# TensorE's expert loop: one width choice per item, three passes looped inside each width's code, six widths from 128 columns, loop head aligned to 16 KB

## The chip, the core and the metric

The kernel runs on one core of a Trainium2 chip. The metric is the device time of one launch in microseconds, the median of three runs. Beside it stands one profiled execution, from which all rows below are read.

## What is computed

One decoder block on 1024 tokens of width 1024 in fp32: a combined projection, four heads of differential attention and four of a chunked mLSTM, an output projection, then a mixture of experts and a final norm. The change touches the mixture of experts alone. Each token picks its top 4 of 32 experts; each expert is a clamped SwiGLU of width 1024:

```python
def expert_block(args):
    rows, e = args
    xb = xt[rows]
    gu = xb @ w_gu[e] + b_gu[e]                      # 1024 -> 2048
    glu = jnp.minimum(gu[:, :D_FF], SWIGLU_LIMIT)
    lin = jnp.clip(gu[:, D_FF:], -SWIGLU_LIMIT, SWIGLU_LIMIT)
    act = glu * jax.nn.sigmoid(SWIGLU_ALPHA * glu) * (lin + 1)
    return act @ w_down[e] + b_down[e]               # 1024 -> 1024
```

The results are weighted by the gates and added to the token rows. The numbers of tokens per expert depend on the data, 4096 in all.

## The kernel before

Everything is one hand-written program for each engine, joined by semaphores; there is no scheduler, so each engine executes what the source says in that order. Some 640 us go into projections, attention, mLSTM and routing. Then comes the loop over items. An item is one expert with up to CAP = 224 of its tokens; experts with more would get further items, up to 18, which are handled by a second loop in which the width is always 224.

TensorE keeps the weights stationary, in blocks of 128x128, and streams the item's token columns. An item is three passes: two halves of gate and up (each gives 512 gate and 512 up features), then the down projection. A pass is 64 matmuls in four slabs of 1 MB of weights, one for each of four slots; every matmul of fp32 operands is executed as two, each with its own weight load, so a pass leaves 128 matmul records in the trace. SyncE (L410) refills a slot as soon as the pass's last matmul on it signals `slab_done`. ScalarE (L1265, L1276, L1259) and VectorE (L1821, L1836, L1839) take the results out of PSUM, add biases and form the activation; VectorE transposes rows in and out (L1774, L1793) and scales the next item's columns (L1782); GpSimd gathers token rows (L560) and adds results to DRAM (L581). These engines always work on the full 224 or 256 columns. Only TensorE looks at the item's true number of tokens, `n_now`: the table `WIDTHS` lists the widths for which the four-slab code exists, and `by_width` walks down a tree of branches (lines 962 to 970) to the narrowest code that holds n.

In `one_pass` (L989 on) a register `phase` tells the pass within the item. L992 and L1001 branch on it: in phase 0 the item's registers are set, in phase 1 the next item's token count is loaded from SBUF (L1002), in phase 2 the registers are moved to the activation's columns. Then `by_width` chooses the code, whose matmul is L1024 with the width w fixed in it, and L1034 advances the count `moved`, against which slots and banks are waited for. The whole is one loop of 96 rounds (L1046), so that head, phase branches and width tree are passed in each of the three passes.

The waits in the four-slab code are those for the columns (`rhs_ready`), the slot (`slot_in`, L1017 and L1021) and the bank (`bank_read`).

## Time and profile before

| | us |
|---|---|
| median of 3 runs | 2265.82 |
| lowest, highest | 2259.61, 2268.32 |
| the profiled execution | 2265.43 |
| its span, first to last instruction | 2263.6 |
| TensorE matmul busy (PE) | 2192.9 |
| VectorE busy (DVE) | 1413.0 |
| ScalarE busy (ACT) | 565.9 |
| matmuls of line L1024, first and last start | 652.5, 2239.0 |

PE is TensorE's matmul side, PEld its weight loads, which run beside matmuls, PEldq and PEq its sequencer's own instructions (branches, register operations). Busy times of PE are those of overlapping records: a record of L1024 lasts 276 ns and more, while the next one starts after 112 to 190 ns. For the pace one therefore takes the time of a stretch over the count of its records. "issue" as the reason of idle time means that the engine waited for nothing that the profile shows.

### The profile page before, as it was taken

The numbers are of one execution on the slowest core, as the hardware profiler recorded it, in microseconds if no ns is written. First come the engines' busy times: TensorE is split into PE (matmuls) and PEld (weight loads), VectorE is DVE, ScalarE is ACT, GpSimd is POOL, SyncE is SP. The second block draws the span as 40 slices with busy tenths as digits, with TensorE's granted clock in tenths as the row PEclk, the third lists the DMA queues.
The fourth block names the chain that finished last, engine by engine and source line by source line (L and its number), as shares of the span: only waits on it lengthen the run. The fifth ranks groups of instructions, "written<-read, shape, count | busy, mean of one in ns | idle before, by whom it ended". The sixth has DMA issues, their size and how long they took to land.

```text
span 2263.6 us, 40201 instructions
## 1 busy us (share of the span) xinstructions
PE 2192.9 (97%) x14677; PEld 1893.8 (84%) x14679; DVE 1413.0 (62%) x2880; ACT 565.9 (25%) x1240; POOL 258.3 (11%) x235
## 2 busy tenths in 40 slices
PE   8999999999978999999999999999999999999996
PEld 4444554566668999999999999999999999999996
DVE  3352231678684777777778677764755566667567
ACT  2122221344311222222222222321221122222123
POOL 1000000121230110111001000110100000001013
PEclk9999999999988999999999999999999999999998
DMA  8000011210165899989989888976976788788688
GB/s 312 34 38 0 0 38 40 98 58 29 67 210 175 282 306 306 304 283 307 312 277 311 282 282 305 311 256 210 304 262 224 235 278 286 244 294 295 232 257 294
DMA packets 244662, 488.92 MB, mean 216 GB/s; under 512 B 24572, under 2 KB 24780, under 8 KB 244452
## 3 DMA queue, kind: packets, MB, share of 16 engines
q1 hardware_dynamic: 223684, 452.48, 57.3%
q0 software_dynamic: 20704, 35.60, 7.1%
q8 instruction: 34, 0.56, 0.1%
q10 hardware_dynamic: 224, 0.16, 0.0%
q14 instruction: 16, 0.13, 0.0%
HBM read 477.67 MB, written 49.63 MB: 233 GB/s over the span
## 4 chain that ended last, share of the span: by engine, by line
PE 92%; DVE 4%; issue 1%; ACT 1%; DMA 1%; POOL 0%; DVEq 0%; SPq 0%; POOLq 0%; ACTq 0%
PE PS L1024 66%; PE PS L664 15%; PE PS L851 5%; PE PS L791 1%; PE PS L824 1%; DVE pairA L1793 1%; PE PS L813 1%; PE PS L870 0%; DMA pairB<-acc_dram 0%; DVE unit L1522 0%; DVE pairA L1839 0%; PE PS L736 0%; DVE unit L1833 0%; PE PS L659 0%; PE PS L637 0%
## 5 line engine op out<-in xcount | busy, mean ns | idle before, releaser
L1024 PE MATMUL PS<-pairA,unit 128*128 x12288 | 1563.1, 290 | 31.3 <-DVE pairA L1839 11.9
L1024 PEld LDWEIGHTS PS<-pairA,unit 128*128 128x128 f32 x12288 | 1554.5, 191 | 40.0 <-issue 39.4
L1774 DVE STREAM_TRANSPOSE unit<-unit 32x512 f32<-32x512 f32 (+1 forms) x512 | 325.5, 636 | 10.3 <-DMA unit<-h_dram,cur_x 3.0
L1793 DVE STREAM_TRANSPOSE pairA<-unit 32x512 f32<-32x512 f32 (+1 forms) x512 | 325.8, 636 | 7.1
L664 PE MATMUL PS<-pairA,unit 128*128 128x512 f32 (+1 forms) x528 | 231.1, 594 | 1.4 <-issue 1.4
L1276 ACT ACTIVATE unit<-PS,cur_b 128x256 f32<-128x256 f32 x256 | 107.5, 471 | 414.9 <-PE PS L1024 414.9
L560 POOL DMA_INDIRECT unit<-h_dram,cur_x x66 | 68.8, 1042 | 1184.4 <-DVE cur_x L1829 1160.5
L664 PEld LDWEIGHTS PS<-pairA,unit 128*128 128x128 f32 (+1 forms) x528 | 97.4, 188 | 116.1 <-issue 115.4
L1259 ACT ACTIVATE unit<-unit 128x512 f32<-128x512 f32 x128 | 80.6, 630 | 453.8 <-DVE unit L1821 453.8
L1265 ACT ACTIVATE unit<-PS,cur_b 128x256 f32<-128x256 f32 x256 | 107.4, 471 | 317.7 <-PE PS L1024 314.2
L1813 DVE COPY cur_b<-b_all 128x24 f32 x32 | 6.7, 209 | 265.2 <-ACT unit L1276 261.3
L1836 DVE TENSOR_SCALAR unit<-unit 128x512 f32<-128x512 f32 x128 | 54.5, 426 | 167.0 <-ACT unit L1265 164.1
L1821 DVE TENSOR_SCALAR unit<-PS,cur_b 128x256 f32<-128x256 f32 x256 | 108.7, 478 | 40.7 <-PE PS L1024 38.6
L581 POOL DMA_INDIRECT acc_dram<-pairA,cur_y x64 | 102.8, 1606 | 211.4 <-ACT pairA L1251 201.0
L664 PE MATMUL PS<-unit,pairA 128*128 128x512 f32 x256 | 112.0, 595 | 0.3 <-ACT unit L1115 0.3
L664 PEld LDWEIGHTS PS<-unit,pairA 128*128 128x128 f32 x256 | 48.0, 190 | 59.5 <-issue 58.2
L1833 DVE TENSOR_TENSOR unit<-unit 128x512 f32<-128x512 f32 x128 | 88.4, 691 | 8.8
L1839 DVE SCALAR_TENSOR_TENSOR pairA<-unit 128x512 f32<-128x512 f32 x128 | 88.7, 693 | 4.4
L1251 ACT ACTIVATE pairA<-pairA,g_now 128x512 f32<-128x512 f32 x128 | 81.6, 715 | 1.8 <-DVE pairA L1793 1.8
L1782 DVE TENSOR_TENSOR pairA<-unit,vec 128x448 f32<-128x448 f32 x128 | 71.4, 620 | 0.0
L1522 DVE CUSTOM_DVE_ANT_0 unit<-PS,unit 128x128 f32<-128x128 f32 (+7 forms) x64 | 48.0, 750 | 29.2 <-PE PS L791 29.2
L1192 ACT ACTIVATE unit<-unit,small 128x128 f32<-128x128 f32 (+7 forms) x64 | 49.4, 772 | 51.5 <-DVE small L1525 51.0
(252 smaller groups left out, 1130.6 us busy)
## 6 DMA issues: line engine op xcount, KB each, us to landing
unit<-in_expert_w_gu_dram SPq DMA_DIRECT2D x256, 1024.0 KB, 5.1
unit<-in_expert_w_down_dram SPq DMA_DIRECT2D x128, 1024.0 KB, 8.2
unit<-in_w_in_dram SPq DMA_DIRECT2D x6, 2048.0 KB, 15.9
pairB<-in_x_dram SPq DMA_DIRECT2D x16, 512.0 KB, 5.9
unit<-in_w_out_dram SPq DMA_DIRECT2D x2, 2048.0 KB, 8.9
h_dram<-pairA SPq DMA_DIRECT2D x8, 512.0 KB, 2.6
acc_dram<-pairB SPq DMA_DIRECT2D x8, 512.0 KB
pairB<-acc_dram SPq DMA_DIRECT2D x8, 512.0 KB, 7.9
```

What stands on the lines that cost most here:

```text
L581: pool.indirect_dma_start(out=acc_dram, out_offset=bass.IndirectOffsetOnAxis(ap=cur_y[:, b:b + 1], axis=0), in_=y_rows[:, b, :], in_offset ...
L664: ins = pe.matmul(ps, lhs, rhs, start=(k == 0), stop=(k == KD - 1))
L851: ins = pe.matmul(ps, (da_mixT, ml_mixT)[k // 4][:, k % 4, P * t:P * t + P], w_o[k // 4][:, k % 4, HALF * half:HALF * half + HALF], start= ...
L1024: ins = pe.matmul(ps[:, ITEM * (j % 2):ITEM * (j % 2) + w], slot_w[s][:, k, P * j:P * j + P], xa_cols[:, ITEM * kd:ITEM * kd + KD * ITEM + ...
L1251: act.activation(half, half, ACT.Identity, scale=g_now[:, q // 2, :]).then_inc(y_evac, 1)
L1265: ins = act.activation(lin_b[:, b, ITEM * j:ITEM * j + ITEM], bank(2 + b)[:, ITEM * j:ITEM * j + ITEM], ACT.Identity, bias=cur_b[:, f:f + 1])
L1276: ins = act.activation(yT[:, 2 * s + j, :], bank(s)[:, ITEM * j:ITEM * j + ITEM], ACT.Identity, bias=cur_b[:, 2 * NF + 2 * s + j:2 * NF + ...
L1774: ins = dve.transpose(cols[:, :, :, 32 * q:32 * q + 32], rows[:, :, :, 32 * a:32 * a + 32])
L1793: ins = dve.transpose(rows[:, :, :, 32 * a:32 * a + 32], cols[:, :, :, 32 * q:32 * q + 32])
L1821: ins = dve.tensor_scalar(glu_t[:, b, ITEM * j:ITEM * j + ITEM], bank(b)[:, ITEM * j:ITEM * j + ITEM], cur_b[:, f:f + 1], LIMIT, ALU.add, ...
L1833: step.do(dve.tensor_tensor(glu_s[:, b, :], glu_t[:, b, :], glu_s[:, b, :], ALU.mult))
L1839: dve.scalar_tensor_tensor(out=actT[:, 2 * c:2 * c + 2, :].rearrange("p j n -> p (j n)"), in0=lin_c[:, b, :], scalar=1.0, in1=glu_s[:, b, ...
```

## The change

Only TensorE's program changes. The table of widths gets six entries, 128, 140, 152, 168, 184 and 224, instead of five, 132, 148, 168, 184 and 224. The register `phase` goes. The outer loop has one round per item, 32 in all: at its head the item's registers are set, the width is chosen once, and inside the code of each width stands a loop of three passes, at whose start one branch sees whether this is the third (then the registers move on to the activation's columns). The next item's token count is loaded in every pass. The columns' half is read from its register in each pass. Before the outer loop stands an alignment: the loader fills up so that the loop's first instruction lies at a multiple of 256 instructions (16 KB). Since the tree still splits off the first width first, the order of the codes in memory is 224, 184, 168, 152, 140, 128.

```diff
--- before.py
+++ after.py
@@ -53,7 +53,7 @@
 LISTS = 2 * (ROUNDS + 1)
 CAP_BITS = 21
 CAP_MUL = (1 << CAP_BITS) // CAP + 1
-WIDTHS = [132, 148, 168, 184, CAP]
+WIDTHS = [128, 140, 152, 168, 184, CAP]
 SLOTS = 4
 NO_ROW = 1 << 20
 
@@ -974,64 +974,63 @@
             turn_early((1, 2, 3))
             place(NT - 1)
             add_rows(NT - 2)
-            n_now, n_next, phase, moved, first_half, all_eight, half, item = (pe.alloc_register(n) for n in (
-                "n_now", "n_next", "phase", "moved", "first_half", "all_eight", "half", "pe_item"))
+            n_now, n_next, moved, first_half, all_eight, half, item = (pe.alloc_register(n) for n in (
+                "n_now", "n_next", "moved", "first_half", "all_eight", "half", "pe_item"))
             pe.wait_ge(items_ready, 1)
             pe.load(n_next, item_n[0:1, 0:1])
             pe.reg_mov(n_now, SEQ)
-            for reg, value in ((moved, 16), (first_half, 4), (all_eight, 0), (half, 0), (phase, 0), (item, 0)):
+            for reg, value in ((moved, 16), (first_half, 4), (all_eight, 0), (half, 0), (item, 0)):
                 pe.reg_mov(reg, value)
             add_rows(NT - 1)
             pe.wait_ge(h2T_ready, 2 * NT)
             pe.wait_ge(place_read, NT)
             pe.wait_ge(b_ready, 2)
 
-            def one_pass(widths):
-
-                p = pe.snap(phase, min_val=0, max_val=2)
-                with pe.If(p < 1):
-                    pe.reg_mov(n_now, n_next)
-                    pe.reg_add(item, item, 1)
-                    pe.reg_add(first_half, all_eight, 2)
-                    pe.reg_add(all_eight, all_eight, 4)
-                    pe.reg_mov(half, 0)
-                    pe.reg_mov(phase, 1)
-                with pe.Else():
-                    nxt = pe.snap(item, min_val=1, max_val=ITEMS)
-                    with pe.If(p < 2):
+            def four_slabs(w):
+
+                block0 = pe.snap(half, min_val=0, max_val=KD * ITEM)
+                for s in range(SLOTS):
+                    side, low = s // 2, s % 2 == 0
+                    if side == 0:
+                        pe.wait_ge(rhs_ready, first_half if low else all_eight)
+                    pe.wait_ge(slot_in[s], moved)
+                    for j in range(4):
+                        ps = bank(2 * side + j // 2)
+                        if low and j % 2 == 0:
+                            pe.wait_ge(bank_read[2 * side + j // 2], moved)
+                        for k in range(4):
+                            kd = k if low else 4 + k
+                            ins = pe.matmul(ps[:, ITEM * (j % 2):ITEM * (j % 2) + w],
+                                            slot_w[s][:, k, P * j:P * j + P],
+                                            xa_cols[:, ITEM * kd:ITEM * kd + KD * ITEM + w][:, bass.ds(block0, w)],
+                                            start=(low and j % 2 == 0 and k == 0), stop=(not low and k == 3),
+                                            skip_group_check=True)
+                        if not low and j == 1:
+                            ins.then_inc(low_bank_done[side], 1)
+                    ins.then_inc(slab_done[s], 1)
+
+            def one_item(widths):
+
+                pe.reg_mov(n_now, n_next)
+                pe.reg_add(item, item, 1)
+                pe.reg_add(first_half, all_eight, 2)
+                pe.reg_add(all_eight, all_eight, 4)
+                pe.reg_mov(half, 0)
+                n = pe.snap(n_now, min_val=0, max_val=SEQ)
+                nxt = pe.snap(item, min_val=1, max_val=ITEMS)
+
+                def three_passes(w):
+
+                    with pe.Fori(0, 3) as p:
+                        with pe.If(p > 1):
+                            pe.reg_add(first_half, all_eight, 2)
+                            pe.reg_add(all_eight, all_eight, 4)
+                            pe.reg_mov(half, KD * ITEM)
                         pe.load(n_next, item_n[0:1, bass.ds(nxt, 1)])
-                        pe.reg_mov(phase, 2)
-                    with pe.Else():
-                        pe.reg_add(first_half, all_eight, 2)
-                        pe.reg_add(all_eight, all_eight, 4)
-                        pe.reg_mov(half, KD * ITEM)
-                        pe.reg_mov(phase, 0)
-                n = pe.snap(n_now, min_val=0, max_val=SEQ)
-                block0 = pe.snap(half, min_val=0, max_val=KD * ITEM)
-
-                def four_slabs(w):
-                    for s in range(SLOTS):
-                        side, low = s // 2, s % 2 == 0
-                        if side == 0:
-                            pe.wait_ge(rhs_ready, first_half if low else all_eight)
-                        pe.wait_ge(slot_in[s], moved)
-                        for j in range(4):
-                            ps = bank(2 * side + j // 2)
-                            if low and j % 2 == 0:
-                                pe.wait_ge(bank_read[2 * side + j // 2], moved)
-                            for k in range(4):
-                                kd = k if low else 4 + k
-                                ins = pe.matmul(ps[:, ITEM * (j % 2):ITEM * (j % 2) + w],
-                                                slot_w[s][:, k, P * j:P * j + P],
-                                                xa_cols[:, ITEM * kd:ITEM * kd + KD * ITEM + w][:, bass.ds(block0, w)],
-                                                start=(low and j % 2 == 0 and k == 0), stop=(not low and k == 3),
-                                                skip_group_check=True)
-                            if not low and j == 1:
-                                ins.then_inc(low_bank_done[side], 1)
-                        ins.then_inc(slab_done[s], 1)
-
-                by_width(n, widths, four_slabs)
-                pe.reg_add(moved, moved, 16)
+                        four_slabs(w)
+                        pe.reg_add(moved, moved, 16)
+
+                by_width(n, widths, three_passes)
 
             def turn_last():
                 for side in range(2):
@@ -1043,8 +1042,9 @@
                                                yT[:, 4 * side + m, P * (q // 2):P * (q // 2) + P], ident[:, :])
                         ins.then_inc(y_ps, 1)
 
-            with pe.Fori(0, 3 * N_EXP):
-                one_pass(WIDTHS)
+            pe.addr_align(256)
+            with pe.Fori(0, N_EXP):
+                one_item(WIDTHS)
             pe.wait_ge(items_ready, 2)
             last = pe.value_load(n_items[0:1, 0:1], min_val=N_EXP, max_val=ITEMS)
             with pe.If(last <= N_EXP):
@@ -1052,8 +1052,7 @@
             with pe.Else():
                 with pe.Fori(N_EXP, ITEMS) as extra:
                     with pe.If(extra < last):
-                        with pe.Fori(0, 3):
-                            one_pass([CAP])
+                        one_item([CAP])
                 turn_last()
```

How the built program's instructions stand on TensorE, at the entry of the loop (the last matmuls of L957 come before it), before:

```order
L957 MATMUL PS<-unit,pairA 128x224 x8
L1046 UNCONDITIONAL_BRANCH
L992 COMPARE_AND_BRANCH
L993 ISA
L992 UNCONDITIONAL_BRANCH
L1001 COMPARE_AND_BRANCH
L1002 ISA
L1002 TENSOR_LOAD item_n
L1001 UNCONDITIONAL_BRANCH
L1005 ISA
L1004 UNCONDITIONAL_BRANCH
L1009 ISA
```

and now:

```order
L957 MATMUL PS<-unit,pairA 128x224 x8
L1045 ISA
L1046 UNCONDITIONAL_BRANCH
L1014 ISA
L1019 ISA
L967 COMPARE_AND_BRANCH x4
L1024 UNCONDITIONAL_BRANCH
L1025 COMPARE_AND_BRANCH
L1026 ISA
L1025 UNCONDITIONAL_BRANCH
L1029 ISA
L1029 TENSOR_LOAD item_n
```

The phase branches are gone, the width branches L967 stand at the head of the item, and the load of `item_n` has moved behind them, into the code of each width (here that of 224).

The end of the loop on TensorE, from the last matmuls of the narrowest width on, before:

```order
L1024 MATMUL PS<-pairA,unit 128x132 x45
L969 UNCONDITIONAL_BRANCH
L1034 ISA
L1046 COMPARE_AND_BRANCH
L1049 TENSOR_LOAD n_items
```

and now:

```order
L1003 MATMUL PS<-pairA,unit 128x128 x45
L1031 ISA
L1024 COMPARE_AND_BRANCH
L969 UNCONDITIONAL_BRANCH
L1046 REGISTER_ALU
L1046 COMPARE_AND_BRANCH
L1049 TENSOR_LOAD n_items
```

The count `moved` is advanced within the width's code, followed by the branch back to the next pass (L1024 of the new source); only then comes the branch back to the head (L1046).

## Rows read from the trace of the kernel before

**Rows 1.** The page: busy time, chain by line, costliest groups (busy us, mean ns | idle).

```profile
PE 2192.9 (97%) x14677; PEld 1893.8 (84%) x14679; DVE 1413.0 (62%) x2880; ACT 565.9 (25%) x1240; POOL 258.3 (11%) x235
...
PE PS L1024 66%; PE PS L664 15%; PE PS L851 5%; PE PS L791 1%; PE PS L824 1%; DVE pairA L1793 1%; PE PS L813 1%; PE PS L870 0%; DMA pairB<-acc_dram 0%; DVE unit L1522 0%; DVE pairA L1839 0%; PE PS L736 0%; DVE unit L1833 0%; PE PS L659 0%; PE PS L637 0%
...
L1024 PE MATMUL PS<-pairA,unit 128*128 x12288 | 1563.1, 290 | 31.3 <-DVE pairA L1839 11.9
```

**Rows 2.** Waits 740 to 2240 us: us in total, times, longest us.

```profile
PE PS L1024 <- DVE pairA L1839: 3.1, 8, 0.6
...
PE PS L1024 <- issue: 3.1, 17, 0.2
...
SPq L410 <- PE PS L1024: 1275.7, 364, 5.5
```

**Rows 3.** Windows, one item each: 132, 148, 168, 224 columns wide.

```profile
core 0: us, PE busy (x) PEld busy (x) DVE busy (x) ACT busy (x) POOL busy (x), PEclk, DMA share, GB/s
774.16:817.88 43.72, 43.53 (x386) 43.34 (x385) 33.29 (x61) 11.68 (x24) 5.28 (x4) 1.00 0.93 304
1129.90:1179.60 49.70, 48.96 (x386) 48.52 (x386) 33.57 (x61) 11.68 (x24) 5.29 (x4) 1.00 0.84 276
1266.90:1322.10 55.20, 55.07 (x387) 54.82 (x386) 33.56 (x61) 11.68 (x24) 5.29 (x4) 1.00 0.77 251
1496.90:1569.60 72.70, 72.70 (x387) 72.70 (x386) 33.55 (x61) 11.68 (x24) 5.28 (x4) 1.00 0.58 194
```

**Rows 4.** Timeline of PE at the loop's start: start, us, group [idle before <-releaser].

```profile
652.47 18.12 PE L1024 MATMUL PS<-pairA,unit 128*128 x128 [7.59 <-issue]
679.41 18.29 PE L1024 MATMUL PS<-pairA,unit 128*128 x128 [8.82 <-DVE pairA L1839]
705.31 18.98 PE L1024 MATMUL PS<-pairA,unit 128*128 x128 [7.60 <-DVE pairA L1782]
724.45 16.37 PE L1024 MATMUL PS<-pairA,unit 128*128 x128 [0.16 <-issue]
```

**Rows 5.** Branches L967 in 642:650, 670:680, 697:703 us: ns min/median/max.

```profile
L967 PEldq COMPARE_BRANCH  x3: 73/4437/4711, 642.9 to 647.8; - x3
...
L967 PEldq COMPARE_BRANCH  x3: 68/232/7974, 670.7 to 678.9; - x3
...
L967 PEldq COMPARE_BRANCH  x3: 73/2987/4719, 697.1 to 702.0; - x3
```

**Rows 6.** The same branches from 730 to 2240 us.

```profile
L967 PEldq COMPARE_BRANCH  x186: 65/202/210, 740.5 to 2224.1; - x186
```

**Rows 7.** DMA queues, 640 to 730 us: the instruction queue of TensorE is q8.

```profile
q8 instruction: 13, 0.21, 1.1%
```

**Rows 8.** The same queue in 0:640 and 2240:2263 us, and on the page, whole span.

```profile
q8 instruction: 19, 0.31, 0.2%
...
q8 instruction: 2, 0.03, 0.6%
...
q8 instruction: 34, 0.56, 0.1%
```

**Rows 9.** Windows of the first three passes.

```profile
652.40:679.40 27.00, 18.12 (x128) 17.90 (x128) 22.26 (x41) 6.45 (x11) 6.73 (x6) 0.82 0.60 202
679.40:705.30 25.90, 18.29 (x128) 18.08 (x128) 16.87 (x30) 2.94 (x6) 2.75 (x2) 0.83 0.47 164
705.30:724.40 19.10, 18.98 (x128) 18.77 (x128) 1.60 (x4) 2.59 (x7) 0.00 (x0) 0.86 0.45 159
```

**Rows 10.** Timelines: weight loads of L870, matmuls of L824.

```profile
456.31 1.86 PEld L870 LDWEIGHTS PS<-rw,pairA 128*128 128x128 f32 x16 [0.76 <-DVE pairA L1582]
...
458.60 1.06 PE L824 MATMUL PS<-unit 128*128 128x128 f32 x8
```

**Rows 11.** L1034 at the end of the first pass.

```profile
L1034 PEldq FUSED_REGOPS  x1: 42/42/42, 668.5 to 668.5; - x1
```

**Rows 12.** Windows: the last item.

```profile
2195.40:2239.10 43.70, 43.51 (x386) 43.32 (x385) 37.22 (x68) 13.04 (x26) 8.54 (x8) 1.00 0.96 331
```

## The prediction

> **What bounds the kernel now.** I read the page first. TensorE is busy for 2192.9 us, 97% of the span, and 66% of the chain that ended last is one line, the matmul of the expert loop, L1024 [rows 1]. The waits, taken from 740 us on, say the same from the other side: TensorE waits 3.1 + 3.1 us at it, and SyncE's weight transfers wait for it to free a slot 1275.7 us in total [rows 2]. So from the second item on, a nanosecond taken from each matmul record, or from the instructions between two passes, comes off the time one for one, while VectorE, ScalarE, GpSimd and the DMA only follow.
>
> Next the price of a column. A matmul of this fp32 kernel has two records, each with its own weight load, so an item (three passes of 64 matmuls) has 384. One item each of four of the five widths stands in [rows 3]. The 224-wide item takes 72.70 us with TensorE busy throughout: 189.3 ns a record. Two cycles of 2.4 GHz for each of 224 columns are 186.7 ns, which leaves 2.6 ns. By that, 384 records cost 43.24 us at 132 columns, 48.36 at 148, and 54.76 at 168; the rows have 43.72, 49.70 and 55.20. What is over, 0.48, 1.34 and 0.44 us, is what the branches and register work between passes cost an item. It is largest at 148 columns, whose code lies behind three branches.
>
> Then the start of the loop, which looks quite different. Before the first pass TensorE stands still for 7.59 us, before the second for 8.82, before the third for 7.60 [rows 4]. The name of VectorE on two of them is no reason to blame it: the width branches L967, normally 0.07 to 0.21 us each [rows 6], took up to 4.7, 8.0 and 4.7 us in just these places [rows 5]. They wait for code: 13 instruction fetches fall between 640 and 730 us, and none in the 1510 us after that: 19 before 640 and 2 after 2240 us make up the page's 34 [rows 7, 8]. The three passes take 27.00 + 25.90 + 19.10 = 72.0 us where 48.4 would do; part of this is a granted clock of 0.82 to 0.86, the mean of stretches at 2.4 and at 1.2 GHz after each standstill [rows 9].
>
> **The change, part by part.** Which item gets which width needs the number of tokens of each expert. They follow from the reference's router on its inputs: 139, 138, 60, 61, 114, 114, 145, 77, 129, 120, 134, 122, 117, 149, 116, 80, 80, 128, 217, 110, 143, 174, 181, 168, 118, 161, 168, 117, 108, 184, 156, 68. No expert is over 224, so there are 32 items, as [rows 1] has it (12288 = 32 x 384). The widths move like this:
> - 139, 138 and 134 go from 148 to 140: 8 columns x 0.833 ns x 384 = 2.56 us each, -7.7 us.
> - 145 and 143 go from 148 to 152: +1.28 us each, +2.6 us.
> - 149 goes from 168 to 152: -5.1 us.
> - 129 goes from 132 to 140, as 128 no longer holds it: +2.6 us.
> - The other 17 items of the old 132 go to 128. By columns alone each would gain 4 x 0.833 x 384 = 1.28 us, 21.8 us in all. I don't believe it. In the router's matmul L870 only 32 columns move, yet its 16 weight loads follow each other at (1.86 - 0.19) / 15 = 111 ns, and L824, which is exactly 128 columns on 128x128 fp32 weights, runs at (1.06 - 0.275) / 7 = 112 ns [rows 10]. So a weight load sets a floor of about 111.5 ns, against 112.6 ns at 132 columns. The gain is 1.1 ns x 384 x 17 = 7.2 us.
> - 168, 184 and 224 stay.
>
> The sum is -14.8 us; with no floor it would be -29.4 us. The Trainium skill has a rule on the other side: TensorE: Matmul & The Clock Gate (the Trainium skill, section "Wait — 56ns, not 53.3ns?") gives N / 2.4 GHz plus about 2.5 ns between matmuls of N columns. The constant agrees with the 2.6 ns of [rows 3]; carried down to 128 columns it says 109.3 ns and the -29.4 us, which L870 and L824 speak against.
>
> *Between the passes.* The phase tests L992 and L1001 and two of three walks down the width tree disappear; a pass now ends in a branch back to its own code. An item passes the head once. There it does what the second pass did before, branches and the load of `item_n` included, and the load now also runs in every pass. The sequencer works ahead of the matmuls (L1034 is done at 668.5 us, the matmuls of that pass end at 652.47 + 18.12 = 670.6) [rows 4, 11], so about 2 us of such work are hidden, and the pass-internal way, with one branch back, one test and one load, is shorter than that. I price an item at 0.45 us over its records, as 132 and 168 have now. That changes nothing for those; for the five items that leave 148 it is 1.34 - 0.45 = 0.9 us each: -4.5 us. The bounds are 0 (the one remaining walk costs as much as three) and -6 us. The cover is the run ahead; if it were gone, 32 heads at some 2 us would cost 60 us, but nothing in the change takes it away.
>
> *Code.* In the built programs the loop has 1375 instruction slots before and 1713 now, without padding. A block of code is 16 KB, 256 slots: 19 fetches go with the some 5000 instructions ahead of the loop [rows 8]. So there are 5.4 blocks before, 6.7 now. From an aligned head these are seven, and at many other phases they would touch eight. The head is in block 0, the body of 140 columns in blocks 4 and 5, that of 128 in 5 and 6; each body lies in two blocks, and its three passes stay there. The first gap should remain: the first item (139) again meets two branches into code not yet there, 4.7 + 4.4 us before, the same now. The second and third gaps came at returns to the head between passes of one item; these returns are gone. They, with the half clock behind them, are 72.0 - 48.4 - (18.12 - 16.37, the slow part of the first pass) = 21.9 us [rows 9]. But the code that the branches waited for there was mostly code fetched once already, shortly before: 13 fetches for a loop of six or seven blocks. The store seems to take blocks in order and to throw away what was put in the wrong place until a whole round has run in order. The new loop has more far jumps in another order: over blocks 1 to 3 in the first items, and into 1 to 3 when 217, 174 and 168 come, which fetches block 2 late. I put this at four more waits of one fetched block each, 4.4 to 4.7 us: 18.5 us. The net is -3 us. The bounds are -21.9 us (nothing fetched twice) and +15 us (eight such waits).
>
> **Sum**, against the profiled execution of 2265.4 us (span 2263.6 us; the median of the runs, 2265.8 us, is practically the same): 2265.4 - 14.8 - 4.5 - 3 = 2243.1 us. What is next behind TensorE doesn't come in: a narrow item moves 304 GB/s with the DMA engines at 0.93 [rows 3], and at 43.3 instead of 43.7 us it would be 307, where another stretch has 331 GB/s [rows 12].
>
> **The rivals.**
> - *The code doesn't stay in store (slower).* Seven blocks, and the one fetched ahead behind the last, make eight. The trace shows only that six or seven stay [rows 8]. If eight don't, the successor of the last block throws out the head's, and every item waits for at least one block: 31 x 4.6 = 143 us, at the worst 31 x 8.0. Time: 2265.4 - 14.8 - 4.5 - 21.9 + 143 = 2367 us or more. For it: the tight fit, and blocks fetched twice even with fewer. Against it: nothing was fetched in 1510 us though all five widths were used. It decides from the first block that has no place. Chance 0.12. The Trainium skill says two different things here. Advanced Engine Details and Errata (the Trainium skill, section "ISA Cache") gives 128 KB on TensorE in lines of 16 KB, thus eight, and the alignment would just do. Runtime: NRT & Kernel Launch (the Trainium skill, section "Instruction fetch mechanics") speaks of a window of two pages, outside which a taken branch stalls for a fetch; that would be this rival, and [rows 8] speak against it.
> - *Nothing is fetched twice.* With the returns inside an item gone, the store fills in order. 2265.4 - 14.8 - 4.5 - 21.9 = 2224 us. For it: later jumps mostly land in blocks just used. Against it: the two repeats before. Chance 0.2.
> - *Settling costs more than it did:* eight or more waits, or slabs that come late after them. 2265.4 - 14.8 - 4.5 + 15 = 2261 us, up to 2285. Chance 0.14.
> - *No floor from the weight loads.* The 17 items gain all 21.8 us: 2243 - 14.6 = 2228.5 us. Against it two lines of the trace. Chance 0.06.
>
> **How the numbers follow.** The forecast, 2243 us, within 2232 to 2262, has 0.48. A measurement of this kernel tells 0.5% (11 us) from no change, so faster is below 2254.5 and slower above 2277. Faster: most of the forecast (0.40), the second and the fourth rival (0.26): 0.66. Same: the forecast's upper edge (0.08) and most of the third rival (0.11): 0.19. Slower: the rest of the third (0.03) and the first (0.12): 0.15. The range goes from 2222 us, the case without repeats, to 2277 us, and leaves out the first rival and the edges.
>
> **What would show it.** In the changed kernel's trace, the start distance of matmul records in a 128-column item: 111.5 ns and an item of 43.3 us (right), 109.3 ns and 42.4 us (no floor). Items of 140 columns at 46.3 us, of 152 at 50.1. One gap of 7 to 11 us before the first pass, none before the second and third. The width branches at their usual 0.07 to 0.21 us but for some four of 3 to 8 us at heads of items, with as many code fetches outside the first 90 us. If instruction fetches go on all through the loop, the first rival holds and the forecast is wrong; if there are none after the first item, the second.

## The result and the profile after

The changed kernel takes **2291.7 us** (median of six executions, 2287.6 to 2305.0) against 2265.9 us of the kernel before beside it: a ratio of 1.0128 (95% interval 1.0111 to 1.0145; ratios and intervals below are meant the same way, each against the kernel before in the same batch). It is slower by 1.3%; the prediction had 2243 us, 2222 to 2277. The profiled execution has a span of 2285.6 us, 22.0 us more than before's 2263.6.

The page after: busy time, the queue of TensorE's instruction fetches (q8), and the matmul of the expert loop, now line L1003 (busy us, mean ns | idle time before them and what ended most of it).

```profile
PE 2187.0 (96%) x14677; PEld 1889.3 (83%) x14679; DVE 1413.9 (62%) x2880; ACT 565.3 (25%) x1240; POOL 258.4 (11%) x235
...
q8 instruction: 43, 0.70, 0.1%
...
L1003 PE MATMUL PS<-pairA,unit 128*128 x12288 | 1556.2, 290 | 61.2 <-issue 59.2
```

Against [rows 1] the matmuls are busy 6.9 us less, so the narrower widths did arrive, but the idle time before them has doubled, from 31.3 to 61.2 us, and nearly all of it ends in "issue": TensorE waits for no other engine, its own sequencer has nothing for it. 43 blocks of code are fetched instead of 34 [rows 8]; a packet of q8 is one block of 16 KB.

Windows of one item each after, 128, 140, 152 and 224 columns wide (columns as in [rows 3]):

```profile
767.90:811.30 43.40, 43.12 (x385) 42.93 (x385) 33.38 (x61) 11.35 (x24) 5.28 (x4) 1.00 0.92 304
1126.90:1173.30 46.40, 46.02 (x384) 45.81 (x384) 33.52 (x61) 11.36 (x24) 5.28 (x4) 1.00 0.87 294
1260.40:1310.40 50.00, 49.83 (x384) 49.60 (x384) 33.48 (x61) 11.28 (x24) 5.28 (x4) 1.00 0.83 273
1484.30:1557.10 72.80, 72.77 (x385) 72.77 (x386) 33.55 (x61) 11.21 (x24) 5.27 (x4) 1.00 0.58 189
```

These are the lengths that were forecast: 43.3, 46.3 and 50.1 us, and 224 columns as before. An undisturbed item is as short as it should be; the loss is elsewhere. The timeline of TensorE at the loop's start (start, us, group, idle before) shows the first place:

```profile
656.62 48.96 PE L1003 MATMUL PS<-pairA,unit 128*128 x384 [12.11 <-issue]
718.56 48.71 PE L1003 MATMUL PS<-pairA,unit 128*128 x384 [12.98 <-issue]
767.85 12.32 PE L1003 MATMUL PS<-pairA,unit 128*128 x108 [0.58 <-issue]
```

The first item's three passes run through, where before stood gaps of 8.82 and 7.60 us between them [rows 4]. But a gap of 12.98 us has come between the first item and the second. The second place lies where before had nothing at all [rows 6, 8]. From 1480 us on, the branches L967 (ns min/median/max), TensorE's waits (us, times, longest) and the instruction queue:

```profile
L967 PEldq COMPARE_BRANCH  x38: 65/68/6062, 1482.6 to 2210.7; - x38
...
PE PS L1003 <- issue: 28.0, 10, 6.3
...
q8 instruction: 12, 0.20, 0.1%
```

In before's trace the same stretch of the loop (1480 to 2239 us) has not one fetch and 0.9 us of such waits:

```profile
PE PS L1024 <- issue: 0.9, 5, 0.2
```

The fetches begin 18 us into the item of 217 rows, the first that is 224 columns wide, and six of the branches that follow take 3.4 to 6.1 us. Five of the six cost more than they take, since TensorE's clock is down behind them; behind the one of 3.81 us at 1836.9 the granted clock stays at 1.00. Windows behind the branch of 4.35 us at 1599.2 and behind the one of 3.42 us at 1655.6 (the granted clock is the figure behind the five busy times):

```profile
1605.00:1608.00 3.00, 2.98 (x12) 2.98 (x13) 2.10 (x3) 0.00 (x0) 0.00 (x0) 0.50 0.06 23
...
1660.30:1678.00 17.70, 17.66 (x95) 17.66 (x96) 8.16 (x17) 1.26 (x2) 2.08 (x2) 0.83 0.37 129
```

0.50 is 1.2 GHz, 0.83 a mixture of both levels.

To say what each part costs I take, for every item, the time from its first matmul record to the next item's, and subtract 384 records at their undisturbed length (2 x width / 2.4 GHz + 2.5 ns, and 111.5 ns at least). What is left over is standstill (for code, and now and then for a slab of weights), slow clock and the work between passes. "Columns" is the sum of what was subtracted, a calculated figure and not a measured one. Items count from 0; "late" stands below for items 18 to 31, which begin at about 1480 us. In us, with the fetches of code from the first matmul of the loop on in brackets, for all kernels of this case but e12 (each from its one profiled execution, which for e3, e5 and e7 is the slowest of its runs):

```
                 widths picked  aligned | start  columns  items 0-1  items 2-17  items 18-31 | last matmul
before              5   pass       no   | 652.5   1545.0  25.1 (11)    9.8 (0)     6.8 (0)   | 2239.0
after               6   item      yes   | 656.6   1530.8  19.7 (7)    12.0 (1)    42.8 (12)  | 2261.7
e1_five             5   item      yes   | 657.8   1545.0  17.3 (7)     9.6 (1)     6.0 (0)   | 2235.6
e2_noalign          6   item       no   | 655.0   1530.8   3.9 (2)    11.4 (0)    20.4 (5)   | 2221.3
e3_chain            6   item      yes   | 664.8   1530.8   5.0 (3)    25.8 (0)    18.0 (0)   | 2244.3
e4_linger           6   item      yes   | 657.2   1530.8  17.8 (7)    13.0 (1)    46.0 (12)  | 2264.6
e5_skip             6   item      yes   | 656.5   1530.8   4.3 (2)    12.9 (0)    56.2 (14)  | 2260.5
e6_chain208         6   item  at 208    | 660.0   1530.8  50.4 (19)  383.2 (138) 112.4 (45)  | 2736.6
e7_off229           6   item  at 229    | 657.4   1530.8   4.9 (2)    11.5 (0)    58.4 (19)  | 2262.9
e8_five130_free     5   item       no   | 654.0   1534.8   5.7 (3)    12.7 (0)     7.3 (0)   | 2214.4
e9_five_free        5   item       no   | 654.4   1545.0   5.2 (3)    10.2 (0)     7.6 (0)   | 2222.3
e10_six_alone       6   pass       no   | 654.3   1530.8  35.0 (11)   12.7 (0)    60.1 (18)  | 2292.8
e11_align_alone     5   pass      yes   | 658.3   1545.0   5.9 (3)     9.8 (0)     7.1 (0)   | 2225.8
e13_walk            6   item      yes   | 668.9   1530.8   3.8 (2)    12.9 (0)     9.3 (0)   | 2225.5
e14_walk130         6   item      yes   | 667.3   1525.9   5.6 (2)    12.0 (0)     7.5 (0)   | 2218.3
```

The first two rows are the account of the change: start +4.1, columns -14.2, items 0 and 1 -5.4, items 2 to 17 +2.2, items 18 to 31 +36.0, which makes +22.7 us at the last matmul; 0.7 us come back behind it. The change of the columns can be checked against measured time in items 2 to 17, where nearly nothing is fetched: together they take 722.7 us before and 716.5 after, 6.3 us less, and the account has -8.5 for their columns and +2.2 for the rest.

### The profile page after: what moved, and what is told of

The parts are those of the page before. It is cut to its first block, busy times and chain, and to the rows that moved or that the text cites. A ratio compares the mean times of both kernels' runs of the same rounds, so it can differ in the third digit from the quotient of the medians.

```text
span 2285.6 us, 40116 instructions
## 1 busy us (share of the span) xinstructions
PE 2187.0 (96%) x14677; PEld 1889.3 (83%) x14679; DVE 1413.9 (62%) x2880; ACT 565.3 (25%) x1240; POOL 258.4 (11%) x235
## 4 chain that ended last, share of the span: by engine, by line
PE 93%; issue 3%; DVE 1%; DMA 1%; ACT 1%; SPq 0%; POOL 0%; POOLq 0%; DVEq 0%; ACTq 0%
PE PS L1003 67%; PE PS L664 15%; PE PS L851 5%; PE PS L791 1%; PE PS L824 1%; DMA pairB<-acc_dram 1%; PE PS L813 1%; PE PS L870 0%; DVE unit L1521 0%; PE PS L736 0%; PE PS L659 0%; PE PS L637 0%; DMA pairB<-in_x_dram 0%; PE PS L957 0%; PE PS L724 0%
## 5 line engine op out<-in xcount | busy, mean ns | idle before, releaser
L1003 PE MATMUL PS<-pairA,unit 128*128 x12288 | 1556.2, 290 | 61.2 <-issue 59.2
L1003 PEld LDWEIGHTS PS<-pairA,unit 128*128 128x128 f32 x12288 | 1549.2, 193 | 68.5 <-issue 68.2
```

What stands on the lines that cost most here:

```text
L1003: ins = pe.matmul(ps[:, ITEM * (j % 2):ITEM * (j % 2) + w], slot_w[s][:, k, P * j:P * j + P], xa_cols[:, ITEM * kd:ITEM * kd + KD * ITEM + ...
```

## The experiments

Blocks are counted from the loop's head: block 0 holds the head, the aligned loop of six widths lies in 0 to 6, the body of 224 columns in 0 and 1, 184 in 1 and 2, 168 in 2 and 3, 152 in 3 and 4, 140 in 4 and 5, 128 in 5 and 6 (from the built program).

### First round: what of the change brings the stalls

After the comparison of the traces I had a theory (A in the expectations that follow): the store has eight places in a ring; whoever enters a block has the next one fetched into the place behind it; a branch to a block that isn't there has it put into the place behind the current one, whatever stands there. The trace shows when a block is fetched, but neither which one nor where it is put, so this is a model. With the order in which the changed kernel visits its blocks it gave 23 fetches in the loop, as many as the trace has from 640 us to the loop's end. The others say that the size decides, or the structure.

**e1_five.**

```diff
-WIDTHS = [128, 140, 152, 168, 184, CAP]
+WIDTHS = [132, 148, 168, 184, CAP]
```

> The changed kernel with the old five widths (132, 148, 168, 184, 224), so 5.6 blocks of loop code instead of 6.7. Theory A (order of the store: it holds eight blocks of 16 KB, a block that is fetched goes behind the one the sequencer runs in, and what stood there is lost, so far jumps in a new order throw out code that is needed): 11 code fetches in the loop, all before 780 us, none from 780 to 2240 us; the waits from the 19th item on, about 42 us, go, the wider code costs 13 us more: 2263 us. Theory B (capacity: seven blocks and the one fetched ahead don't fit, five widths do): the same 2263 us. Theory C (the new loop form, not its code size, is what costs): the late waits stay, 2290 us or more.

2264.5 us (ratio 1.0006, 0.9991 to 1.0021), as A and B both had it, so this run doesn't tell them apart; C is refuted. With one width less the late fetches are gone, 6.0 us over the columns in items 18 to 31 as in before, although the structure and the alignment are the changed kernel's. Its waits from 1480 to 2200 us:

```profile
PE PS L1003 <- issue: 3.0, 7, 0.7
```

The first item's stall stays.

**e2_noalign.**

```diff
-            pe.addr_align(256)
```

> The changed kernel without the alignment before the loop: the head then lies some 165 instructions into a block and the loop touches eight blocks instead of seven. Theory A: 18 fetches in the loop instead of 23 and fewer late branches that wait (items 20 to 24 instead of 20 to 32), no padding to run through before the loop: about 2270 us. Theory B: with eight blocks and one ahead even less fits, so fetches go on in nearly every item: over 2300 us. Theory C: 2285 us, the padding's few us less.

**2247.9 us** (ratio 0.9932, 0.9909 to 0.9956): without its alignment the changed kernel is faster than before, and 44 us faster than with it. None of the figures foresaw that, mine being 22 us too high. The loop touches eight blocks now instead of seven and stalls less, so a mere count of blocks, by which B had over 2300 us, is refuted. It isn't free of late stalls either: five late fetches come in items 18 to 23, with branches of 4.4 and 3.6 us ahead of items 20 and 21, the first two of the five items that theory A named. Of the 18 fetches that A gave the loop, however, only 11 came.

**e3_chain.**

```diff
-                near = 1 if widths[0] == WIDTHS[0] else len(widths) // 2
+                near = len(widths) - 1
```

> The changed kernel with the tree of width branches made a chain: n over 184, else over 168, else over 152 and so on, so that the branches walk through the blocks in the order in which they lie in memory. Same six widths, same seven blocks, aligned. Theory A: 7 fetches in the loop, none after the first item, so both the reload in the second item (16 us) and the late waits (42 us) go; up to five taken branches per item instead of one to three cost 0.2 us each, some 20 us over all items: 2254 us. Theory B: the same bytes don't fit, the fetches stay: 2290 us or more, with the longer chain rather 2310 us.

The widths are tried one after the other from the widest down; each test stands at the head of the body that it chooses, so whoever wants the narrow code passes all blocks. 2266.2 us (1.0014, 0.9999 to 1.0029). There is no late fetch, with the same seven blocks, but the tests cost a narrow item about 1.1 us more, and the loop starts 8 us later. The seven fetches are what A said, the time is 12 us above its figure. Two waits of over 2 us are left in items 24 and 27, and they are not for code: the sequencer stands 2.50 and 2.21 us at L1000, and what ends both waits is the landing of a slab of weights. The first of them, too, has 3.4 us at a granted clock of 0.50 behind it.

**e4_linger.**

```diff
             pe.addr_align(256)
+            for _ in range(6):
+                pe.load(n_next, item_n[0:1, 0:1])
```

> The changed kernel with six loads of a register (0.3 us each) between the alignment and the loop, so that TensorE's sequencer stays in the head's block for about 2 us before its first far branch and the next block is under way by then. Theory A: the first far block then goes behind it, nothing has to be loaded again in the second item: 18 fetches in the loop instead of 23, TensorE's gap between item 1 and 2 (13 us) falls under 1 us, the late waits stay; 2291.7 - 16 + 2 = 2278 us. Theory B: 23 fetches or more, 2293 us.

2291.8 us in two executions, as the changed kernel (1.0127), with the same fetches. But the edit didn't do what it was meant to. Of the six loads only one stands in the trace:

```profile
L1047 PEldq TENSOR_LOAD <-item_n x1: 487/487/487, 648.3 to 648.3; - x1
```

The first slow branch comes at 649.4 instead of 648.5 us, so the sequencer stayed 0.9 us longer in the head's block and not some 2 us. That 0.9 us change nothing is shown; whether 2 us would, as A says, was not tested.

### Second round: is it the place of the code?

**e5_skip.** The alignment fills the rest of the block ahead of the loop with instructions that do nothing, and the changed kernel runs through them. Its trace has 92, within 6.7 us:

```profile
L1045 PEldq NOP  x92: 13/13/13, 641.2 to 647.9; - x92
```

```diff
-            pe.addr_align(256)
+            pe.addr_align(256, max_nops=0)
```

> The changed kernel with its padding branched over instead of executed (the 92 padding instructions were executed between 641.15 and 647.88 us of the changed kernel's span, about 71 ns each). Theory A, the padding costs what it takes: the loop's first matmul comes at 650 us instead of 656.6 and the time falls by 6 to 7 us, to 2285. Theory B, the padding runs beside the fetch of the loop's first blocks, which would be waited for otherwise (without any alignment the loop starts at 655.0, only 1.6 us earlier): the loop starts at 654 to 656 and the time is 2289 to 2292. In both, the late stalls stand where they stood in the changed kernel, since no block lies elsewhere.

The branch over the padding is there (one, at 642.8 us) and the loop's counter is set at 643.2 instead of 647.9 us, but the first matmul comes at 656.5 us, as before the edit (656.6). So B on this point: the padding ran beside fetches that are waited for in any case. The time, however, is 2274.8 us, with ten executions from 2266.9 to 2286.3, which neither theory had. The profiled one is the slowest of them: its first items are clean (4.3 us) and its late ones worse than the changed kernel's (56.2 us, 14 fetches), though not one instruction lies elsewhere. So the addresses alone don't decide what is fetched late. That it is how the first fetches fell in time is the nearest explanation; no run tests it by itself.

**e6_chain208.** e3_chain, moved by 208 instructions:

```diff
-            pe.addr_align(256)
+            pe.addr_align(256, offset=208)
```

> Descending chain of widths as in e3_chain, but the loop's head at instruction 208 of its 16 KB block, so that the code touches eight blocks instead of seven. Theory R (eight places in a ring; entering a block fetches the block behind it into the next place; a branch to a block that isn't there puts it into the next place): the block behind the last one of the loop, fetched ahead for nothing, takes the place of the head block, so that nearly every item's end branches to a block that isn't there: about 36 missed branches and 129 fetches in the loop instead of 8, each miss 3.3 to 4.5 us and up to 3 us of half clock behind it: 2380 to 2460 us. Theory C (what counts is whether the loop's blocks fit into eight): eight fit, nothing is fetched again, 2264 to 2275 us.

**2763 us**, in one execution. The loop touches blocks 0 to 7 now. TensorE between 800 and 1010 us:

```profile
801.85 44.83 PE L1003 MATMUL PS<-pairA,unit 128*128 x384 [24.39 <-issue]
869.75 45.00 PE L1003 MATMUL PS<-pairA,unit 128*128 x384 [23.07 <-issue]
937.59 45.20 PE L1003 MATMUL PS<-pairA,unit 128*128 x384 [22.84 <-issue]
```

and the page, with the branches L967 from 730 us on:

```profile
q8 instruction: 227, 3.72, 0.6%
...
L1003 PE MATMUL PS<-pairA,unit 128*128 x12288 | 1597.6, 295 | 493.5 <-issue 491.2
...
L967 PEldq COMPARE_BRANCH  x140: 70/3096/5968, 775.4 to 2686.8; - x140
```

At the ends of the first 18 items TensorE stands for 17 to 29 us, but for one: seven to eleven blocks are fetched in each of these items (three in the last), one after the other, and the median branch takes 3.1 us. Same instructions, same order, 497 us more than e3_chain. Eight blocks don't stay when the items walk through them; seven do. That a ninth, fetched ahead for nothing, is what is too much fits the nine fetches that most of the first narrow items have, but isn't shown by itself. C is refuted. R is right in kind and far too mild: it had 129 fetches in the loop where 207 came, and 2460 us at most.

Advanced Engine Details and Errata (the Trainium skill, section "ISA Cache") gives TensorE 128 KB in lines of 16 KB, thus eight; the same section has "Only 2 cache lines!" beside it, which the seven blocks that stay in e3 contradict. Eight places agree with e3 and e6 if one of them goes to the block ahead. Runtime: NRT & Kernel Launch (the Trainium skill, section "Instruction fetch mechanics") has a taken branch stall whenever its target isn't in the current window of two pages; in e1_five the branches go from block 0 to block 4 for more than 1400 us and nothing is fetched, so this does not hold here.

**e7_off229.**

```diff
-            pe.addr_align(256)
+            pe.addr_align(256, offset=229)
```

> The changed kernel with its loop starting at instruction 229 of a 16 KB block instead of 0: same code, same order, eight blocks touched as without the alignment (instruction 165). Theory R: the fetches come out at 33 in the loop, with missed branches after items 19, 20, 22, 23, 24, 26, 27, 28 and 30 about (11 in all after the first item, against 6 in the changed kernel): 2305 to 2325 us. Theory U (an unaligned loop is good and an aligned one bad, whatever the cause): like the kernel without the alignment, 2246 to 2255 us. Theory C (eight blocks fit): the same as U.

2282.6 us (1.0077, 1.0045 to 1.0110), four executions from 2276.3 to 2289.4. The loop is as little aligned as in e2_noalign, which starts at instruction 165 of its block, and has 58.4 us late instead of 20.4 (in the slowest of the four, the profiled one). So it isn't alignment against none; each place of the code has its own stalls. R's figure was 22 us too high (24 fetches, not 33), U's 27 too low.

**e8_five130_free.**

```diff
-WIDTHS = [128, 140, 152, 168, 184, CAP]
+WIDTHS = [130, 146, 168, 184, CAP]
...
-            pe.addr_align(256)
```

> Five widths (130, 146, 168, 184, 224), passes looped inside each width, no alignment. 130 columns take 110.8 ns by columns, below the 111.5 ns that the 128-column records show, so 130 costs what 128 costs and takes item 8 (129 rows) in; the columns' sum of the loop is 1534.9 us against 1544.96 of before's widths and 1530.8 of the six. Theory R puts no missed branch behind the second item with this size and start: overhead as in e1_five behind its second item (15.7 us) and as in e2_noalign ahead (4 us), loop from 655 to 2209, span 2233 to 2237, time 2235 to 2239. Theory U/C: the same, as the code is smaller. If the second walk through the blocks that e1_five showed after its first item (12.4 us) comes here too: 2247 to 2251.

**2241.4 us** (0.9914, 0.9883 to 0.9946), the fastest of all, 19.6 us below the kernel before beside it. L967 and the waits from 1480 to 2200 us:

```profile
L967 PEldq COMPARE_BRANCH  x34: 65/169/210, 1544.0 to 2170.0; - x34
PE PS L1003 <- issue: 2.7, 6, 0.7
```

No branch over 0.21 us. It gives up 4.1 us of the six widths' columns and has nothing of their stalls. The forecast of R was 2 us too low.

### Third round: each part alone

**e9_five_free**, the loop over passes alone (e8 with before's widths):

```diff
-WIDTHS = [130, 146, 168, 184, CAP]
+WIDTHS = [132, 148, 168, 184, CAP]
```

> One part alone: the width picked once per item with the three passes looped inside, but before's five widths and no alignment. Column sum 1544.96 us, 10.1 more than e8_five130_free (2241.36), everything else the same code in the same places. Theory R (no missed branch behind the second item, seven blocks): 2250 to 2253 us, a gain of 10 to 13 us over before that comes from the first item's two stalls of 8 to 9 us and the half clock behind them. Rival (the loop over passes gives nothing, e8's gain is its widths): 2258 to 2263.

2252.6 us (0.9956, 0.9937 to 0.9974), 11 us above e8, whose columns are 10.1 less. The time is in R's range. The gain over before, 8.9 us between the medians, lies where it was said to, in the first items: 5.2 instead of 25.1 us. The later start (1.9 us) takes some of it back.

**e10_six_alone**, the widths alone, on the kernel before:

```diff
-WIDTHS = [132, 148, 168, 184, CAP]
+WIDTHS = [128, 140, 152, 168, 184, CAP]
```

> One part alone: six widths in before's structure (the width picked again in each pass, no alignment, eight blocks touched). Columns give 14.2 us. Theory R: eight blocks and a ninth fetched ahead don't fit into eight places, so that from item 18 on branches miss again, 5 to 10 times at 5 to 6 us each beside before's first item: 2275 to 2305 us. Theory W (six widths are what they are by columns, the stalls of the changed kernel come from its structure or its alignment): 2251 to 2256.

**2324.8 us** (1.0289, 1.0246 to 1.0332). Its page:

```profile
q8 instruction: 51, 0.84, 0.2%
...
L1024 PE MATMUL PS<-pairA,unit 128*128 x12288 | 1569.1, 291 | 77.7 <-issue 74.5
```

W is refuted: with neither the loop over passes nor the alignment the sixth width brings 60.1 us of late stalls, 20 us more than the range of R, and 35.0 us in the first items.

**e11_align_alone**, the alignment alone, on the kernel before:

```diff
+            pe.addr_align(256)
             with pe.Fori(0, 3 * N_EXP):
                 one_pass(WIDTHS)
```

> One part alone: before with its loop aligned to a 16 KB block, nothing else (six blocks touched). Theory R: behind the first item no block is fetched; the padding runs beside fetches and costs 1 to 4 us at the loop's start, the first item's stalls are 12 to 24 us as in before: 2258 to 2270 us. Theory U (the alignment is what costs, some 40 us as between the changed kernel and e2_noalign): 2290 to 2310.

**2251.7 us** (0.9943, 0.9923 to 0.9963), below both ranges. TensorE in the first item:

```profile
658.27 19.03 PE L1024 MATMUL PS<-pairA,unit 128*128 x128 [12.88 <-issue]
678.17 16.37 PE L1024 MATMUL PS<-pairA,unit 128*128 x128 [0.87 <-issue]
```

The gap ahead of the second pass is 0.87 us, where before has 8.82 [rows 4], with the very same returns to the head. The alignment, which costs the changed kernel 44 us, gives before 10 (difference of the medians) to 13 (by the ratio).

**e12_floor96** tests the floor of a record. On e2_noalign, the body of the narrowest width multiplies 96 columns instead of 128:

```diff
             def four_slabs(w):
+                u = 96 if w == 128 else w
...
-                            ins = pe.matmul(ps[:, ITEM * (j % 2):ITEM * (j % 2) + w],
+                            ins = pe.matmul(ps[:, ITEM * (j % 2):ITEM * (j % 2) + u],
```

(and the columns of the second operand likewise)

> e2_noalign whose narrowest code multiplies only 96 of its 128 columns (columns 96 to 127 of the 17 items that run in it are left out of the product, so those rows' outputs are not the reference's). Theory F (a matmul of this kernel is never shorter than loading its 128 by 128 float32 weights, 111.5 ns): a record stays at 111.5 to 111.7 ns, an item at 43.4 us, the time at 2248. Theory N (the records follow the columns down): 82.5 ns a record inside a slab, which would leave such an item to its transfers at about 38 us or less, and the time at 2060 to 2160.

2248.1 us in one execution; e2_noalign has 2247.9. A window of one such item:

```profile
1380.80:1424.20 43.40, 43.12 (x385) 42.96 (x385) 33.35 (x61) 11.70 (x25) 5.28 (x4) 1.00 0.92 309
```

43.40 us for 384 records, as the 128 columns take in e2_noalign and in the changed kernel; inside the slabs a record starts 111.7 ns after the other in all three, so it isn't the transfers that hold them. A quarter fewer columns gives nothing, and N is refuted. The floor goes with the load of 128 x 128 float32 weights, which is what these records share with those of L870, 111 ns apart with 32 columns moved [rows 10]. The rule of N / 2.4 GHz + 2.5 ns (the Trainium skill, TensorE: Matmul & The Clock Gate, section "Wait — 56ns, not 53.3ns?") would have 82.5 ns for such a record, at the two cycles a column that [rows 3] show; that section doesn't count the load, so it doesn't hold here.

### Fourth round: why seven blocks don't stay

e3_chain kept seven blocks, the changed kernel did not. Either the order in which the first items bring them in decides, or the chain's habit of passing all of them each time.

**e13_walk.**

```diff
-                near = 1 if widths[0] == WIDTHS[0] else len(widths) // 2
+                near = 1 if widths[0] == WIDTHS[0] else len(widths) - 1
```

> The changed kernel (six widths, aligned) with one change in the tree of branches: 128 columns are reached by one branch as there, the others by a descending chain, so that the first item (139 rows) passes the blocks 1 to 5 in order before its passes. Theory O (what decides is that the blocks come in once, in order; the late fetches come from block 2, which the changed kernel's first items jump over): no code fetch behind 720 us, items 18 to 31 within 10 to 18 us over their columns instead of 42.8, the loop starts at about 665 us as in e3_chain: 2244 to 2256 us. Theory D (e3_chain is free of late fetches only since every item walks the blocks and so keeps them; a jump from block 0 to blocks 5 and 6 throws something out): late fetches as in the changed kernel, 2285 to 2300.

**2253.0 us** (0.9947, 0.9928 to 0.9965), 39 us below the changed kernel. The same from 1480 to 2200 us:

```profile
L967 PEldq COMPARE_BRANCH  x46: 65/169/210, 1480.2 to 2181.2; - x46
PE PS L1003 <- issue: 5.8, 10, 1.4
```

Its page, whole span:

```profile
q8 instruction: 27, 0.44, 0.1%
```

O, then. The 17 items of 128 columns jump from block 0 to block 5 as in the changed kernel, which by D should have thrown something out. The items with wider code take another way, down the chain; the first item does so through blocks 1 to 5 in order, and from the second item's start (717.8 us) to the end of the loop nothing is fetched, so later walks can have brought nothing in. Nor is it luck in time as in e5_skip, as far as executions tell: the ten of e5_skip and the six of the changed kernel all lie above 2266 us, the four of this kernel between 2252.1 and 2255.4.

How the order does it is the model's account. In the changed kernel the first items jump from 0 to bodies in 4 to 6 by way of 3. Block 2 isn't needed until the item of 217 rows has its successor fetched (the fetch at 1502.6 us); by the model it comes into a full ring, out of order, and throws out a block in use, whose return throws out the next: twelve fetches and six waits up to the end. The price of the walk is the start, 12.3 us later.

**e14_walk130** is e13_walk with widths 130, 140, 150, 168, 184, 224:

```diff
-WIDTHS = [128, 140, 152, 168, 184, CAP]
+WIDTHS = [130, 140, 150, 168, 184, CAP]
```

> e13_walk with widths 130, 140, 150, 168, 184, 224. The columns' sum falls from 1530.8 to 1525.9 us (the 129-row item into the 130-column code, whose records cost the floor of 111.5 ns; three items from 152 to 150). Theory O: 4.9 us below e13_walk, 2239 to 2251, about even with e8_five130_free (2241.36). Theory D: 2280 to 2295.

2246.7 us (0.9917, 0.9899 to 0.9935): 6.3 us less than e13_walk, 4.9 by its columns. By its ratio it is level with e8_five130_free.

## Why the prediction was wrong

*Widths: right.* Forecast -14.8 us with a floor of 111.5 ns; the account has -14.2, which is calculated with the same floor. What is measured bears it out: the 128-column item takes 43.40 us, 140 columns 46.40, 152 columns 50.00, as forecast, and e12 shows that the floor is one.

*Between the passes: wrong in sign, small.* Forecast -4.5 us, of which 1.8 fall to items 2 to 17. There stand +2.2. The items that leave 148 columns did gain (134 rows: from 1.36 to 0.65 us over its records), but the narrow ones, priced at 0.45 us as before, take 0.6 to 1.9. What failed is the sentence that one way over the head is hidden as the second pass's was: in items 2 to 17 the time lost between passes inside an item fell from 6.8 to 0.8 us, as meant, but that between items rose from 0.2 to 8.7. And "what is next behind TensorE doesn't come in" was not quite so: item 7 stands 1.28 us at L1000 for a slab of weights, the last item 1.90.

*Code: this is the step that failed.* Forecast -3 us, with bounds of -21.9 and +15; measured +34.7 (start +4.1, items 0 and 1 -5.4, items 18 to 31 +36.0). Three things in it:
- "These returns are gone" gave -21.9 us. Inside the first item the gaps are gone, as said. But new ones have come at the first return to the head, now between items 0 and 1, as if the store's settling had only moved there: branches of 8.9 and 3.3 us with five fetches, then 5.5 us of matmuls at half clock, which costs 2.8. Of the 21.9 us 5.4 came. e11 shows from the other side that the returns weren't the cause: there they all remain and the gaps are gone.
- The start got no term at all. The loop begins 4.1 us later, after a gap of 12.11 us where "7 to 11" was forecast, and by e5_skip it isn't the padding's execution.
- "Four more waits ... 4.4 to 4.7 us" should have been eight: two ahead of the second item, six behind 1480 us. Eight were my bound. But the late ones cost 36.0 / 6 = 6.0 us each on average, as slow clock stands behind five of them and one lasts 6.1 us by itself.

*The rivals.* "The code doesn't stay in store" had the right mechanism, blocks that throw each other out again long after the start, and the wrong form: I let it cost every item 4.6 us or none. Both ends exist, e6 (497 us over e3) and e13 (none), and the changed kernel lies between, since only the wide items disturb a loop that otherwise runs in few blocks. "Settling costs more" was next to the truth with its upper figure, 2285 us, at a chance of 0.14 and "the rest of the third (0.03)" for slower. "Nothing is fetched twice" (2224) and "no floor" (2228.5) did not occur.

*Where the argument broke.* Against the first rival I had held that nothing was fetched in 1510 us though all five widths were used [rows 8]. That is evidence for that loop, with five widths. I carried it over to one with a width more, in which the first items leave a block out, although the text itself names that block ("which fetches block 2 late"); I priced its fetch and not what it throws out.

*Left open.* What decides the first item's stall: 4 to 6 us over two items in e2, e3, e5, e7, e8, e9, e11, e13 and e14, 17 to 20 in the changed kernel, e1 and e4, 25 in before, 35 in e10, 50 in e6. It goes neither with the alignment nor with the structure nor with the number of widths, and e5 against the changed kernel shows it change with 4.7 us of time ahead of the loop. So the part of the miss that lies ahead of item 2 has no cause shown. Open, too, is the exact rule by which blocks are replaced: the ring as I wrote it down gives the number of the changed kernel's fetches, the place of e2's late waits and the absence of late fetches in e1, e3, e9, e11 and e13; for e6, e7 and the first items of e2 its counts are wrong, and it can't tell e5 from the changed kernel.

## What to carry to other kernels

Where an engine's loop has one body for each case, its code has a capacity, and one case more can cost more than it saves: here a loop ran freely with seven blocks of 256 instructions, if its first rounds had brought them all in, and not with eight. So count the blocks before the columns, and look at every jump that leaves one out. Whether a loop sits well shows in three lines of the trace, the instruction queue's packets by stretch, the longest branch, and the matmul's idle time put down to "issue"; after every change of the code's size they must be read again, since an alignment that saved 10 to 13 us in one version cost 44 in another. And a matmul narrower than its weight load is free to be wider: 130 columns in place of 128 cost nothing.

## What the runs showed of the hardware that I had not expected

- The same instructions, shifted by 208 places, took 2763 us (one execution) instead of 2266 (e6, e3).
- In the changed kernel a branch that waits for code takes 3.1 to 4.4 us when one block is fetched, 6.1 with two and 8.9 with three. Behind five of the six late ones matmuls run at 1.2 GHz (granted clock 0.50) for 3 us and more.
- A record of a float32 matmul with 128 x 128 weights takes about 111.7 ns at 96 and at 128 columns (e12, the changed kernel).
- The time of one kernel can scatter over 13 to 20 us where late items fetch code (e5_skip, e7_off229, e10_six_alone, the changed kernel), against 1.3 us in e11_align_alone, which fetches none late. It is no rule: e2_noalign has late fetches and scatters over 5 us, the kernel before has none and scatters over 11.
